# Second mixer's end with tiles 256 columns apart, and fewer parted products

## What is computed

```
h = concatenate([meta_b, x], axis=1)                       # 16 + 256 tokens
for l in range(DEPTH):                                     # DEPTH = 2
    h = h + 0.5 * swiglu(rmsnorm(h, ffn1_norm[l]), ...)
    h = h + hybrid_mixer(rmsnorm(h, mix_norm[l]), ...)
    h = h + 0.5 * swiglu(rmsnorm(h, ffn2_norm[l]), ...)
h = rmsnorm(h, final_norm)                                 # h[:, 16:] goes on
...
def hybrid_mixer(u, w_in, w_attn_out, conv_w, ..., w_conv_out, w_out):
    q, k, v, a, b, g_sb, g_conv = jnp.split(u @ w_in, IN_SPLITS, axis=-1)
    y_sb = stick_breaking_attention(q, k, v) @ w_attn_out
    y_conv = conformer_conv(a, b, ...) @ w_conv_out
    return (jax.nn.sigmoid(g_sb) * y_sb + jax.nn.sigmoid(g_conv) * y_conv) @ w_out
def swiglu(x, w_gate, w_up, w_down):
    return (jax.nn.silu(x @ w_gate) * (x @ w_up)) @ w_down  # 1024 -> 2816 -> 1024
```

## Time and profile before

| | |
|---|---|
| median of 3 runs | 2172.21 us (2171.7 to 2172.26) |
| profiled execution, its own time | 2172.23 us |
| its span | 2170.4 us |
| PE busy | 2159.0 us (99%) |
| DVE busy | 1473.0 us (68%) |
| ACT busy | 1202.2 us (55%) |
| POOL busy | 283.9 us (13%) |

### The profile page before, as it was taken

The page is one execution under the profiler, slowest core; times in us unless marked ns, Lnnn a source line. Parts: engine busy times, 40 slices in busy tenths (PEclk is TensorE's granted clock), DMA queues, the critical chain, the costliest instruction groups (busy, mean ns, idle before and its releaser), DMA issues.

```text
span 2170.4 us, 48317 instructions
## 1 busy us (share of the span) xinstructions
PE 2159.0 (99%) x18139; PEld 2141.7 (99%) x18139; DVE 1473.0 (68%) x2242; ACT 1202.2 (55%) x1752; POOL 283.9 (13%) x328
## 2 busy tenths in 40 slices
PE   8999999999999999999999999999999999999999
PEld 8999999999999999999999999999999999999999
DVE  6655998665566579876657657976656745686663
ACT  6444786544444368755555546865445535565552
POOL 0001661100100136220020011010010010101000
PEclk9999999999999999999999999999999999999999
DMA  6555435556455554455656655356656655445664
GB/s 233 176 192 167 163 118 175 175 174 198 153 181 186 182 165 142 149 177 193 205 180 194 200 188 170 117 184 191 207 173 195 209 178 180 161 158 195 193 217 131
DMA packets 100401, 386.57 MB, mean 178 GB/s; under 512 B 11312, under 2 KB 12464, under 8 KB 100304
## 3 DMA queue, kind: packets, MB, share of 16 engines
q1 hardware_dynamic: 99648, 383.89, 53.7%
q0 software_dynamic: 368, 1.26, 0.2%
q10 hardware_dynamic: 288, 0.12, 0.0%
HBM read 384.18 MB, written 1.05 MB: 177 GB/s over the span
## 4 chain that ended last, share of the span: by engine, by line
PE 91%; DVE 6%; ACT 2%; issue 1%; DMA 0%; SPq 0%; ACTq 0%; DVEq 0%
PE bank L423 28%; PE bank L416 28%; PE bank L424 28%; DVE wlo L439 2%; DVE bank L1702 1%; PE bank L1056 1%; PE bank L1058 1%; PE bank L1057 1%; ACT whi L432 1%; PE bank L1103 0%; PE bank L770 0%; DVE proj L1688 0%; PE bank L947 0%; PE bank L950 0%; PE bank L949 0%
## 5 line engine op out<-in xcount | busy, mean ns | idle before, releaser
L416 PE MATMUL bank<-u,whi 128*128 128x256 f32 (+2 forms) x3776 | 1062.6, 281 | 7.3 <-DVE u L477 7.3
L423 PE MATMUL bank<-u,whi 128*128 128x256 f32 (+1 forms) x3776 | 1062.1, 281 | 0.0
L424 PE MATMUL bank<-u,wlo 128*128 128x256 f32 (+1 forms) x3776 | 1060.0, 281 | 0.0
L439 DVE TENSOR_TENSOR wlo<-raw,whi 128x1024 fp32r<-128x1024 f32 (+1 forms) x677 | 892.7, 1321 | 186.1 <-ACT whi L432 185.5
L432 ACT ACTIVATE whi<-raw 128x1024 fp32r<-128x1024 f32 (+1 forms) x677 | 743.5, 1112 | 192.3 <-PE bank L424 172.0
L416 PEld LDWEIGHTS bank<-u,whi 128*128 128x128 f32 x3776 | 711.3, 188 | 8.5 <-DVE wlo L439 7.2
L423 PEld LDWEIGHTS bank<-u,whi 128*128 128x128 f32 x3776 | 711.3, 188 | 0.9 <-issue 0.2
L424 PEld LDWEIGHTS bank<-u,wlo 128*128 128x128 f32 x3776 | 711.1, 188 | 0.0
L416 PE MATMUL bank<-hid,whi 128*128 128x256 f32 (+1 forms) x1408 | 394.2, 280 | 0.0
L423 PE MATMUL bank<-hid,whi 128*128 128x256 f32 (+1 forms) x1408 | 394.2, 280 | 0.0
L424 PE MATMUL bank<-hid,wlo 128*128 128x256 f32 (+1 forms) x1408 | 394.2, 280 | 0.0
(11 more groups left out here) (297 smaller groups left out, 2190.8 us busy)
## 6 DMA issues: line engine op xcount, KB each, us to landing
raw<-w SPq DMA_DIRECT2D x552, 512.0 KB, 3.3
raw<-w SPq DMA_DIRECT2D x128, 704.0 KB, 4.8
h<-xT SPq DMA_DIRECT2D x4, 272.0 KB, 5.6
outT<-h SPq DMA_DIRECT2D x8, 128.0 KB, 5.0
consts<-cst POOLq DMA_DIRECT2D x1, 576.0 KB, 5.0
dist<-cst POOLq DMA_DIRECT2D x1, 192.0 KB, 2.8
rdist<-cst POOLq DMA_DIRECT2D x1, 192.0 KB, 3.7
sgain<-small POOLq DMA_DIRECT2D x1, 145.5 KB, 5.4
```

The source lines that it names most:

```text
L416: pe.matmul(out[:, cut:cols], w, x[:, cut:cols], start=first, stop=False, skip_group_check=True)
L423: pe.matmul(out, w_h, x_lo, start=False, stop=False, skip_group_check=True)
L424: return pe.matmul(out, w_l, x_hi, start=False, stop=last, skip_group_check=True)
L439: dve.tensor_tensor(weights(1, n), raw[:, n % RING, 0:COLS[n]].rearrange("p (k c) -> p k c", c=128), weights(0, n), ALU.subtract).then_inc ...
```

## The change

In the second mixer's end (`l` = 1) the moving tiles are written and read 256 columns apart (`mixed_at`, `attended_at`), the weight tiles stand 128 apart without the shift of 16 columns, and three products are parted anew. Elsewhere partings go: panel 2's in the five feed-forward blocks of 256 columns, one of the two at the end of the second mixer's `w_in`, and six of thirteen in retention. The first mixer is as before.

```diff
-CUTS = (0, 252, 128, 0)
-BEHIND_TERMS = [(0, 1), (0, 2), *((t, c) for t in range(1, RT_HEADS + 1) for c in (0, 1)), (RT_HEADS, 5), (RT_HEADS + 1, 1), (RT_HEADS + 1, 2)]
+CUTS = (0, 252, 0, 0)
+BEHIND_TERMS = [(0, 1), *((t, 1) for t in range(1, RT_HEADS + 1)), (RT_HEADS, 5), (RT_HEADS + 1, 1)]
...
+        def mixed_at(l, part, k):
+
+            if l == 0:
+                return qk[:, KD * part + k, :]
+            at = KD * T * part + SEQ * k
+            return qk[:, :, :].rearrange("p a t -> p (a t)")[:, at:at + SEQ]
+
+        def attended_at(l, part, k, rows=slice(0, 128)):
+            buf = (ao_hi, ao_lo)[part]
+            if l == 0:
+                return buf[rows, k, :]
+            return buf[:, :, :].rearrange("p a t -> p (a t)")[rows, SEQ * k:SEQ * k + SEQ]
...
-            step = GAP_STEP if in_mixer_end(n) else 128
-
-            at = META if BASE[LAST_MIX]["P"] + 20 <= n < BASE[LAST_MIX + 1]["P"] else 0
+            step = GAP_STEP if in_first_mixer_end(n) else 128
+
+            at = META if BASE[LAST_MIX]["P"] + 20 <= n < BASE[LAST_MIX]["P"] + IN_PANELS else 0
...
-                    in_panel(j, N2, CUTS[1] if N2 == SEQ and j > FIRST_PANELS + 4 * PAIRS else 0)
+                    in_panel(j, N2, CUTS[1] if N2 == SEQ and j == FIRST_PANELS + 4 * PAIRS + 1 else 0)
...
-                                mm = products(pe, bank[g % MIX_BANKS][:, 0:N2], n, 4 * ff + k, x_hi,
-                                              x_lo, k == 0, k == 3)
+                                mm = products(pe, bank[g % MIX_BANKS][:, 0:N2], n, 4 * ff + k, x_hi,
+                                              x_lo, k == 0, k == 3,
+                                              CUTS[1] if N2 == SEQ and (p, ff, k) == (0, 1, 0) else 0)
...
-                        mm = products(pe, bank[MIX_OUT[f]][:, 0:N2], P + 44 + f, k, qk[:, k, W2], qk[:, KD + k, W2],
-                                      k == 0, k == KD - 1)
+                        mm = products(pe, bank[MIX_OUT[f]][:, 0:N2], P + 44 + f, k, mixed_at(l, 0, k), mixed_at(l, 1, k),
+                                      k == 0, k == KD - 1, CUTS[1] if N2 == SEQ and f == 2 and k == 0 else 0)
```

More of the change, by code:

```diff
@@ L146, with in_first_mixer_end @@
 HID_PLACE = {0: (24, 0), 2: (24, 0), 3: (24, 0), 5: (24, 0), 7: (24, 0), 9: (24, 0), 10: (24, 0), 12: (24, 0)}
-CUTS = (0, 252, 128, 0)
-BEHIND_TERMS = [(0, 1), (0, 2), *((t, c) for t in range(1, RT_HEADS + 1) for c in (0, 1)), (RT_HEADS, 5), (RT_HEADS + 1, 1), (RT_HEADS + 1, 2)]
-def in_mixer_end(n):
-    return any(BASE[y]["P"] + IN_PANELS <= n < BASE[y + 1]["P"] for y, kind in enumerate(PHASES) if kind == "mix")
+CUTS = (0, 252, 0, 0)
+BEHIND_TERMS = [(0, 1), *((t, 1) for t in range(1, RT_HEADS + 1)), (RT_HEADS, 5), (RT_HEADS + 1, 1)]
+def in_first_mixer_end(n):
+    y = PHASES.index("mix")
+    return BASE[y]["P"] + IN_PANELS <= n < BASE[y + 1]["P"]
 STREAMED = [BASE[PHASES.index("da")]["P"] + j for j, (part, _) in enumerate(DA_PANELS) if part == 2]
@@ L819, in mix @@
                                     pe.wait_ge(co_ready, CH * l + k + 1)
-                                x_hi, x_lo = ((qk[:, k, W2], qk[:, KD + k, W2]),
-                                              (ao_hi[:, k, W2], ao_lo[:, k, W2]))[part]
+                                x_hi, x_lo = ((mixed_at, attended_at)[part](l, i, k) for i in range(2))
                                 mm = products(pe, bank[g % MIX_BANKS][:, 0:N2], n, 4 * ff + k, x_hi,
-                                              x_lo, k == 0, k == 3)
+                                              x_lo, k == 0, k == 3,
+                                              CUTS[1] if N2 == SEQ and (p, ff, k) == (0, 1, 0) else 0)
                         mm.then_inc(panel_used, 1)
@@ L1254, in co_hi @@
                     act.wait_ge(ysilu, CH * l + c + 1)
-                    act.activation(qk[:, c, W2], proj[:, A_SLOT + c, W2], ACT.Copy).then_inc(co_hi_ready, 1)
+                    act.activation(mixed_at(l, 0, c), proj[:, A_SLOT + c, W2], ACT.Copy).then_inc(co_hi_ready, 1)
                 def log_terms(hd):
@@ L1286, in out_hi @@
                     act.wait_ge(o_full, H + hd + 1)
-                    act.activation(ao_hi[rows, hd // 2, :], bank[5][rows, 0:T], ACT.Copy).then_inc(ao_hi_ready, 1)
+                    act.activation(attended_at(l, 0, hd // 2, rows), bank[5][rows, W2], ACT.Copy).then_inc(ao_hi_ready, 1)
                 for p in range(PAIRS):
@@ L1342, in mix @@
                         act.wait_ge(m_done, KD * l + f + 1)
-                        act.activation(qk[:, f, W2], proj[:, G_SLOT + f, W2], ACT.Copy).then_inc(m_hi_ready, 1)
+                        act.activation(mixed_at(l, 0, f), proj[:, G_SLOT + f, W2], ACT.Copy).then_inc(m_hi_ready, 1)
                 act_split(act, P + 43 + RING)
@@ L1768, in out_lo @@
                     dve.wait_ge(ao_hi_ready, H + hd + 1)
-                    dve.tensor_tensor(ao_lo[rows, hd // 2, :], bank[5][rows, 0:T], ao_hi[rows, hd // 2, :],
+                    dve.tensor_tensor(attended_at(l, 1, hd // 2, rows), bank[5][rows, W2], attended_at(l, 0, hd // 2, rows),
                                       ALU.subtract).then_inc(ao_ready, 1)
@@ L1815, in mix @@
                     dve.wait_ge(co_hi_ready, CH * l + c + 1)
-                    dve.tensor_tensor(qk[:, KD + c, W2], cacc[:, c, W2], qk[:, c, W2],
+                    dve.tensor_tensor(mixed_at(l, 1, c), cacc[:, c, W2], mixed_at(l, 0, c),
                                       ALU.subtract).then_inc(co_ready, 1)
@@ L1845, in mix @@
                         dve.wait_ge(m_hi_ready, KD * l + f + 1)
-                        dve.tensor_tensor(qk[:, KD + f, W2], proj[:, G_SLOT + f, W2], qk[:, f, W2],
+                        dve.tensor_tensor(mixed_at(l, 1, f), proj[:, G_SLOT + f, W2], mixed_at(l, 0, f),
                                           ALU.subtract).then_inc(m_ready, 1)
```

## The result

The changed kernel takes 2191.03 us (median of 6 runs, 2190.09 to 2191.48) against 2172.15 us (6 runs, 2171.7 to 2174.17): a ratio of 1.0085 with a 95% interval of 1.0075 to 1.0095, slower. The profiled execution took 2191.44 us with a span of 2189.6 us, 19.2 more than the earlier trace rows.

The account below looks back on a forecast made before the run. The prediction took TensorE, 99% busy, as the bound, so the spacing of matmul starts counts. Its terms, 20.6 - 0.55 - 1.0 - 0.2 = +18.8 us on 2172.23, gave 2191.0 us, range 2174 to 2200 us.

Parts of the forecast that it names:

- The term that decides: Feed-forward blocks: without panel 2's parting three stay slow to their end, +20.6 us; five partings fewer save 0.55 us.
- Two paces, told by the record's duration: TensorE's same matmul runs steadily at 113.33 or 117.75 ns; a record of 276 or 281 ns tells which.
- The norm toggles: At norms before blocks: entered fast, the pace is left slow; entered slow, left fast; panel 1's parting seems not to decide.
- Nothing inside a stretch changes the pace: Within a stretch, loops, waits and operand changes leave the pace; only something odd between, a norm's matmul or parting, switches it.
- Which blocks: Feed-forward blocks at 1614 and 1990 and one of those at 954 and 1134 turn slow; 1433 stays fast.
- The mixer's end: Second mixer's end: new tile places bring the fast pace, -1.0 us, between -1.4 and 0; part may become bank waits.
- Retention: Retention: six partings go, some panels may run slow; -0.2 us, between -0.7 and +0.1.
- Rival 5: Whole kernel: one pace only, placement and partings don't move it; nine partings fewer, -1.0 us, 2171.2 us; chance 0.02.

Follow-up runs that it names:

- experiment 1: The changed kernel with panel 2's parting at column 128 back in the five feed-forward blocks; 2170.92 us.
- experiment 8: The changed kernel with panel 2's parting at 128 back and `u` at 32, 0 and 16 columns instead of 48 in stages 7, 10, 12; 2187.24 us, one run.
- experiments 1 to 7 and 9 to 10: All follow-up versions but experiment 8: the changed kernel or the kernel before with partings or parts of the change varied; medians from 2169.99 to 2191.69 us.
- experiment 6: The changed kernel with the feed-forward blocks' parting behind the norm at column 128 instead of 252; 2175.75 us, the profiled run 2168.89.
- experiment 2: The kernel before with panel 2's parting removed from the feed-forward blocks, all else as before; 2191.69 us.
- experiment 3: The kernel before with the second mixer's part of the change alone, panel 2's and retention's partings as before; 2170.94 us, -0.95 against the kernel before.

## Why the prediction was right, point by point

**The term that decides.** Right. 20.6 us for three slow blocks, less 0.55: 20.1 by experiment 1. The slow pace passes through loops and down projections, for which there was no row before.

**Two paces, told by the record's duration.** Right, for tiles at their usual places; experiment 8 shows other paces at others. The spans of the changed kernel, the kernel before and experiments 1 to 7 and 9 to 10, each less its excess, agree within 1.9 us while they themselves differ by 22.8.

**The norm toggles.** Half right. In the profiles of all runs with `u` at 48, a block's single norm matmul (stage 9's, beside which TensorE waits, left aside) entered fast was left slow 33 times out of 33, with or without a parting at 252 behind it; only a parting at 128 directly behind it changed that. Entered slow it was left fast in 9 of 11, not always: in the changed kernel stage 5 was entered slow (281 before 953.3) and left slow. The double norm of stage 7 follows no such rule; entered fast it was left fast in five of six (partings at 128 left aside).

**Nothing inside a stretch changes the pace.** Wrong in one place. Where the second mixer's `w_in` ends and its end begins, the tile that streams changes from `u` to `qk` and the weight tiles' place by 16 columns, with no norm, parting or wait between (the starts are 113 to 122 ns apart). In all nine profiles with the new layout the pace turned there: from slow to fast in four, from fast to slow in five. L438 in the changed kernel and in experiment 6:

```profile
L438 PE MATMUL bank<-u,wlo x8: 280/282/282, 902.0 to 904.5; 128*128 128x256 f32 x8
L438 PE MATMUL bank<-qk,wlo x3: 277/277/279, 905.2 to 905.8; 128*128 128x256 f32 x3
...
L438 PE MATMUL bank<-u,wlo x9: 276/276/277, 901.0 to 903.8; 128*128 128x256 f32 x9
L438 PE MATMUL bank<-qk,wlo x3: 281/281/281, 904.1 to 904.8; 128*128 128x256 f32 x3
```

The change from `u` to `hid` leaves either pace as it is, which is all that the sum needed.

**Which blocks.** One of three named wrong. I had 10, 12, and one of 5 and 7. Stage 9, whose norm is followed by a wait of about 0.46 us, came out slow, where the eight other profiles without a parting at 128 there have it fast, and so stage 10, entered slow, came out fast. The number held because a block slow to its end hands the next norm a slow entry; that it was just three was partly luck: experiment 2, with the same partings in the blocks, has executions from 2185.6 to 2193.9.

**The mixer's end.** -1.0 was forecast and experiment 3 gives -0.95, but the agreement is luck: its interval is 0.2% (4 us) wide, and in the traces the stretch behind the wait gained 0.24 us in the changed kernel, 0.69 in experiment 3 and 1.14 in experiment 1, by which half was slow. In the changed kernel the gain came up to 929.06, and the second parting at 252 didn't bring it back. Part of it did turn into waits on DVE, as the prediction had it might: 0.27 us at the bank at 926.21 and 0.07 at 929.06, with DVE busy 13.13 of 15.00 us.

**Retention.** -0.2 against -0.17, which the interval of 0.2% can't tell from nothing.

**Rival 5.** Experiment 8 moved nothing but where tiles stand and got 113.3, 117.8, 118.7 and 120.0 ns for one shape at one clock. The Trainium skill, "TensorE: Matmul & The Clock Gate", section "Step-by-step: what each phase is for", has the two reads on ports of their own, with the load taking nothing from the running matmul. The four paces of experiment 8 don't agree with the rule as the prediction drew it from there, that placement can't move the pace. Whether the load of weights is what takes the time, no run here shows.

## What to carry to other kernels

A matmul stream can have more than one steady rhythm for the same instructions, and what comes in between (an odd matmul, a wait of a tenth of a microsecond, a change of tiles) chooses; so read the pace per stretch, from starts, before costing a change by instruction counts. An instruction that looks redundant may be what ends the bad rhythm, and its price (0.11 us) must be set against the length of what follows (1560 matmuls at 4.42 ns). When executions fall into groups, look for the place where the rhythm can turn, and try the cure behind it.

## What the runs showed that was not expected

- Tiles moved in experiment 8 left aside, a parting at 128 ended the slow pace in 18 of 18 places that met it slow; one at 252 in 4 of 18. Both load the same weights twice. Directly behind a norm one at 128 left the fast pace in 17 of 17, of which eleven are at single norms without a wait, where it would have been slow otherwise. In experiment 8, with `u` at 32, 0 and 16, a parting at 128 ended none of the three longer paces.
- A wait of 0.03 to 0.11 us in the middle of a stretch turned the pace in some executions and not in others. On DVE's tiles for the output projection it did so in five of eight profiles (929.06 in the changed kernel; not at 928.20 in experiment 6), on the splits in stage 7 in two of six, and with it 5.7 us (1164.73 in experiment 2; not in the changed kernel, 1171.27 to 1171.46, fast on both sides).
- At 32, 0 and 16 columns the stretches behind the parting never ran at 113.3 ns, and each down projection behind them, `hid` at its old place, did (1256, 1743 and 2123 us on).
